# First norm of a two-layer diffusion backbone: token sums from the loaded x, root and reciprocal on 128x5, modulation by halves, first projection in parts

## The reference, cut to what matters

```
def adaln(cond, w, b):
    return jnp.split(jax.nn.silu(cond) @ w + b, 6, axis=-1)

def rms_norm(x, g):
    xf = x.astype(jnp.float32)
    xf = xf * lax.rsqrt(jnp.mean(xf * xf, axis=-1, keepdims=True) + EPS)
    return (xf * g.astype(jnp.float32)).astype(x.dtype)

def latent_layer(x, mod, cache, rows, cols, p):
    sh1, sc1, g1, sh2, sc2, g2 = mod
    h = rms_norm(x, p['norm1']) * (1 + sc1) + sh1
    ...
    x = x + g1 * (mixed @ p['w_out'])
    return channel_mlp(x, sh2, sc2, g2, p), (na_k, na_v, ckv, kpe, sk, sv)
```

## Time and profile before

| | us |
|---|---|
| median of 3 runs | 1737.93 |
| lowest, highest | 1737.55, 1741.01 |
| the profiled execution, its time | 1741.36 |
| its span in the trace | 1739.1 |
| mean granted TensorE clock, share of full speed | 0.966 |

### The profile page before, as it was taken

One profiled execution on the slowest core, in us unless ns is written; L12 is line 12 of the kernel. 1 busy time (PEld: TensorE's weight loads), 2 busy tenths in 40 slices (PEclk: granted clock), 3 DMA queues, 4 the chain that ended last, 5 costly groups with the idle time before them and its releaser, 6 DMA issues.

```text
span 1739.1 us, 28317 instructions
## 1 busy us (share of the span) xinstructions
PE 1610.1 (93%) x11686; PEld 1489.9 (86%) x11686; DVE 949.3 (55%) x1480; ACT 664.1 (38%) x1045; POOL 148.3 (9%) x107
## 2 busy tenths in 40 slices
PE   5878897899999999999988799978999999999998
PEld 3755895589999999999967569946999999999998
DVE  3653346856555545654584433497566456554553
ACT  4554533753422322232244454357433222332231
POOL 1002102520000000000010030064000000000000
PEclk9898998999999999999999899989999999999999
DMA  9440443311222222223534205341222222222211
GB/s 312 156 144 1 72 142 103 112 47 52 76 94 70 69 81 73 73 73 116 191 106 135 85 1 119 106 155 50 73 74 73 73 73 73 73 73 73 91 55 61
DMA packets 150856, 160.14 MB, mean 92 GB/s; under 512 B 16390, under 2 KB 132808, under 8 KB 150728
## 3 DMA queue, kind: packets, MB, share of 16 engines
q1 hardware_dynamic: 150024, 158.13, 29.7%
q10 hardware_dynamic: 576, 0.16, 0.0%
q0 software_dynamic: 128, 0.05, 0.0%
HBM read 153.41 MB, written 4.65 MB: 91 GB/s over the span
## 4 chain that ended last, share of the span: by engine, by line
PE 78%; DVE 11%; ACT 6%; issue 3%; DMA 1%; ACTq 0%; DVEq 0%; SPq 0%
PE ps L1552 33%; PE ps L1895 26%; PE ps L1645 10%; PE ps L1617 2%; PE ps L1669 2%; PE ps L1532 1%; DVE extrema L1306 1%; PE ps L1578 1%; ACT pt_c L788 1%; DVE extrema L1289 1%; PE ps L1722 1%; PE ps L1700 1%; DMA ada_own<-in_w_ada 1%; DVE mod L1147 1%; DVE w_lo L1134 1%
## 5 line engine op out<-in xcount | busy, mean ns | idle before, releaser
L788 ACT ACTIVATE w_hi<-w_raw 128x2048 fp32r<-128x2048 f32 (+1 forms) x90 | 169.9, 1887 | 333.8 <-PE ps L1552 324.3
L1348 DVE SCALAR_TENSOR_TENSOR xT<-ps,mod,xT 128x128 f32<-128x128 f32 (+2 forms) x432 | 190.0, 440 | 195.8 <-PE ps L1552 183.9
L1134 DVE TENSOR_TENSOR w_lo<-w_raw,w_hi 128x2048 fp32r<-128x2048 f32 (+1 forms) x90 | 203.1, 2257 | 140.4 <-ACT w_hi L788 138.9
L1895 PE MATMUL ps<-xa_hi,w_hi 128*128 128x320 f32 (+1 forms) x1024 | 236.1, 312 | 0.0
L1895 PE MATMUL ps<-xa_lo,w_hi 128*128 128x320 f32 (+1 forms) x1024 | 235.2, 311 | 0.0
L1895 PE MATMUL ps<-xa_hi,w_lo 128*128 128x320 f32 (+1 forms) x1024 | 235.1, 311 | 0.0
L1552 PE MATMUL ps<-z_hi,w_hi 128*128 128x320 f32 x1024 | 233.7, 310 | 0.9 <-DVE xT L1348 0.9
L1552 PE MATMUL ps<-z_lo,w_hi 128*128 128x320 f32 x1024 | 233.4, 309 | 0.0
L1552 PE MATMUL ps<-z_hi,w_lo 128*128 128x320 f32 x1024 | 233.3, 309 | 0.0
L1106 ACT ACTIVATE z_relu<-z_relu,sink_shift 128x128 f32<-128x128 f32 (+1 forms) x128 | 72.2, 564 | 307.0 <-DVE z_relu L1452 304.9
L1895 PEld LDWEIGHTS ps<-xa_hi,w_hi 128*128 128x128 f32 x1024 | 173.5, 189 | 0.3
(11 more groups left out here) (241 smaller groups left out, 2364.4 us busy)
## 6 DMA issues: line engine op xcount, KB each, us to landing
w_raw<-in_mlp_w SPq DMA_DIRECT2D x64, 1024.0 KB, 5.2
ada_own<-in_w_ada SPq DMA_DIRECT2D x54, 512.0 KB, 4.5
w_raw<-in_w_in SPq DMA_DIRECT2D x14, 1024.0 KB, 7.8
ada_mix<-in_w_ada SPq DMA_DIRECT2D x21, 512.0 KB, 7.8
ada_room<-in_w_ada SPq DMA_DIRECT2D x15, 512.0 KB, 8.9
w_raw<-in_w_out SPq DMA_DIRECT2D x8, 768.0 KB, 5.3
ada_first<-in_w_ada SPq DMA_DIRECT2D x6, 512.0 KB, 9.1
x_in<-in_x_sample SPq DMA_DIRECT2D x1, 2048.0 KB, 8.6
```

Source lines behind the costliest of these rows:

```text
L788: do(nc.scalar.activation(out, in_, ACT.Copy), sem)
L1134: do(V.tensor_tensor(w_lo[:, n % 2, 0:w], w_raw[:, n % 2, 0:w], f32(w_hi[:, n % 2, 0:w]), ALU.subtract), w_lo_ready)
L1348: do(V.scalar_tensor_tensor(dst, src, gate[:, m:m + 1], dst, ALU.mult, ALU.add), sem if last else None)
L1895: last = M.matmul(bank(b + a_, s1 - s0), w[r][:, k, c:c + P], x[:, k, s0:s1], start=k == 0 and q == 0, stop=k == KC - 1 and q == 2)
```

## The change

In layer 0 ACT squares each token tile of x as it was loaded (128 tokens by 1024 channels) with the sum along the row, so `tok_rstd` (128x5) holds each token's sum; no squares of `xT`, no additions and no matmul with ones are left there. In layer 1 the squares stay, but PE takes the partial sums as weights against one column of ones, 10 matmuls of 1 column. Mean, root and reciprocal then run on 128x5. PE spreads the result over the partitions (`spread_rstd`, 6 matmuls of a broadcast column against the identity), and ACT copies it out (`take_rstd`).

The 16 units are taken in the order scale 0 to 3, shift 0 to 3, scale 4 to 7, shift 4 to 7, with two PSUM banks for the sums in turn. h of chunks 0 to 3 waits for the first eight units alone; units 12 to 15 run between chunk 1 and chunk 2 of the projection, their turn between chunk 2 and chunk 3. The first weights are loaded before the ninth unit. The projection's banks are others, and the four units that followed it now stand behind the first tile of ckv. The diff, cut to its core:

```diff
-CQ_BANKS = (0, 1, 3, 7, 2)
+ADA_GROUPS = (2, 0, 3, 1)
+CQ_BANKS = (4, 5, 0, 6, 7)
...
+        FIRST_TICKS = [(None, ("unit", k)) for k in range(6)] + [(("turn", 0), ("unit", 6)), (None, ("unit", 7)), (("turn", 1), None)]
+        FIRST_TICKS += [(None, ("unit", k)) for k in range(8, 12)] + [(("turn", 2), None)]
+        FIRST_TICKS += [(None, ("unit", k)) for k in range(12, 16)] + [(("turn", 3), None)]
...
-            load_adas(0, range(AFTER_X))
-
-            sp.wait_ge(t_done, KC)
+            load_adas(0, range(8))
+            load_weights(0)
+            load_adas(0, range(8, AFTER_X))
+
+            sp.wait_ge(t_done, trans_ix.at[("x", KC - 1)] + 1)
+            sp.wait_ge(x_squared, NT)
             load_adas(0, range(AFTER_X, 16))
-            load_weights(0)
+            load_weights(1)
...
# ACT
+            def take_rstd(l):
+                i = acc_ix.at[(l, "rstd")]
+                act.wait_ge(m_done, i + 1)
+                do(nc.scalar.activation(rstds[0][:, :].rearrange("p (a n) -> p a n", a=2), acc_view(i), ACT.Copy), m_act)
+            def first_norm(l):
+                load_sqrt()
+                if l:
+                    for c in range(KC):
+                        act.wait_ge(y_read, (l * GROUPS - 1) * KC + c + 1)
+                        square_x(2 * l, c)
+                    ada_ticks(48 * l, range(8))
+                    root_x(2 * l)
+                else:
+                    ada_ticks(0, range(4))
+                    root_x(0)
+                take_rstd(l)
+                if l == 0:
+                    ada_ticks(0, range(4, 8))
+                    split_hi(0)
+                ada_ticks(48 * l, range(8, 13))
+                h_halves(2 * l, range(3))
+                ada_ticks(48 * l, range(13, 19))
+                h_halves(2 * l, range(3, KC))
...
-                act.wait_ge(acol_ready, nrm + 1)
                 for c in chunks:
+                    act.wait_ge(acol_ready, 3 * l + 1 + c // 4)
+                    act.wait_ge(mod_ready, 12 * l + 2 + 2 * (c // 4))
...
+            def square_tokens(t):
+                do(nc.scalar.activation(x_sq[:, :], x_in[:, t, :], ACT.Square, accum_out=tok_rstd[:, t:t + 1]), x_squared)
...
# DVE
             for l in range(DEPTH):
                 U = 45 * l
+                if l == 0:
+                    mean(0)
+                    invert(0)
+                ada_ticks(48 * l, range(7))
+                scales(2 * l, 0, 4)
                 if l:
                     mean(2 * l)
-                    ada_ticks(48 * l, range(6))
                     invert(2 * l)
-                    ada_ticks(48 * l, range(6, 18))
+                ada_ticks(48 * l, range(7, 9))
+                if l == 0:
+                    split_lo(0)
...
                 for c in range(KC):
+                    if c == 4:
+                        ada_ticks(48 * l, range(9, 14))
+                        scales(nrm, 4, 4)
+                    if c == 6:
+                        ada_ticks(48 * l, range(14, 19))
...
# POOL
-                pool.wait_ge(rstd_ready, nrm + 1)
+                pool.wait_ge(m_act, acc_ix.last_reader(acc_ix.at[(l, "rstd")])[1])
...
# PE
+            def first_norm(l):
+                if l:
+                    ada_ticks(48 * l, range(8))
+                    begin_acc((l, "sum1"))
+                    sums(l, "sum1")
+                    ada_ticks(48 * l, range(8, 11))
+                    pe.wait_ge(y_read, did["y"])
+                    spread_rstd(l)
+                    ada_ticks(48 * l, range(11, 14))
+                else:
+                    ada_ticks(0, range(6))
+                    spread_rstd(0)
+                    ada_ticks(0, range(6, 14))
+                project_cq(l, 45 * l, range(2))
+                ada_ticks(48 * l, range(14, 18))
+                project_cq(l, 45 * l, range(2, 3))
+                ada_ticks(48 * l, range(18, 19))
+                project_cq(l, 45 * l, range(3, KC))
...
-                project_cq(l, U)
+                first_norm(l)
+                project(l, U + 1, "ckv", range(1))
+                pe.wait_ge(p_read, proj_at[(l, "cq", NT - 1)] + 1)
+                pe.wait_ge(ada_reduced, 12 * l + 4)
                 ada_ticks(late, late_ticks(l, 1))
-                project(l, U + 1, "ckv")
+                project(l, U + 1, "ckv", range(1, NT))
```

More of the change, by code:

```diff
@@ L810, in ada_tick @@
                         act.wait_ge(ada_turned, u // 4)
-                    copy(ada_row[:, :], bank(ada_banks(first)[0]), ada_rows)
+                    copy(ada_row[:, :], bank(ada_acc_bank(first, unit[1])), ada_rows)
             def ada_ticks(first, ks):
@@ L1164, in mean @@
                 rstd = rstds[which]
-                i = acc_ix.at[(l, ("sum1", "sum2")[which])]
+                if which == 0:
+                    if l:
+                        i = acc_ix.at[(l, "sum1")]
+                        dve.wait_ge(m_done, i + 1)
+                        do(V.tensor_reduce(tok_rstd, bank(acc_banks(i), 2 * NT).rearrange("p (a t) -> p t a", a=2), AX_X, ALU.add),
+                           m_dve)
+                    else:
+                        dve.wait_ge(x_squared, NT)
+                    do(V.tensor_scalar(tok_rstd, tok_rstd, 1.0 / D, EPS, ALU.mult, ALU.add), mean_ready)
+                    return
+                i = acc_ix.at[(l, "sum2")]
                 dve.wait_ge(m_done, i + 1)
@@ L1591, in sums @@
                 rstd = rstds[nrm % 2]
+                if which == "sum1":
+                    out = bank(acc_banks(acc_ix.at[(l, which)]), 2 * NT)
+                    for a_, (x, ready, count) in enumerate(((rstd, sum_used, (KC - 2) * nrm), (sq[:, (KC - 1) % 2], sq_ready, KC * nrm))):
+                        pe.wait_ge(ready, count)
+                        for t in range(NT):
+                            at0 = NT * a_ + t
+                            last = M.matmul(out[:, at0:at0 + 1], x[:, P * t:P * t + P], ones[:, 0:1], start=True, stop=True,
+                                            skip_group_check=True)
+                    last.then_inc(m_done, 1)
+                    return
                 out = acc_view(acc_ix.at[(l, which)])
-                for x, ready, count in ((rstd[:, :], sum_used, (KC - 2) * (nrm + 1)),
-                                        (sq[:, (KC - 1) % 2, :], sq_ready, KC * (nrm + 1))):
+                for x, ready, count in ((rstd[:, :], sum_used, (KC - 2) * nrm),
+                                        (sq[:, (KC - 1) % 2, :], sq_ready, KC * nrm)):
                     pe.wait_ge(ready, count)
@@ L1599, in sums, with spread_rstd, project_cq @@
                 last.then_inc(m_done, 1)
-            def project_cq(l, n):
+            def spread_rstd(l):
+                begin_acc((l, "rstd"))
+                pe.wait_ge(tok_ready, l + 1)
+                b = acc_banks(acc_ix.at[(l, "rstd")])
+                for t in range(NT):
+                    for s, e in ((P * t, P * t + P),) if t != 2 else ((P * t, HALF), (HALF, P * t + P)):
+                        last = M.matmul(bank(b + s // HALF)[:, s % HALF:s % HALF + e - s],
+                                        tok_rstd[:, t:t + 1].broadcast_to([P, P]), ident[:, s - P * t:e - P * t],
+                                        start=True, stop=True, skip_group_check=True)
+                last.then_inc(m_done, 1)
+            def first_norm(l):
+                wait_read(trans_ix, did["t"] - 1, t_act, t_dve)
+                wait_read(trans_ix, did["t"] - 2, t_act, t_dve)
+                if l:
+                    ada_ticks(48 * l, range(8))
[5 more added lines that the diff above has]
+                    ada_ticks(48 * l, range(11, 14))
+                else:
+                    ada_ticks(0, range(6))
[6 more added lines that the diff above has]
+                project_cq(l, 45 * l, range(3, KC))
+            def project_cq(l, n, ks):
                 s = n % 2
```

146 lines of the change are left out of this document (62 added, 84 removed).

## The result

The changed kernel takes 1744.98 us (median of 19 runs, 1741.2 to 1750.06), the kernel before beside it 1737.93 (19 runs, 1734.55 to 1742.18). The ratio is 1.0035, 95% interval 1.0026 to 1.0044: about 6 us slower. The forecast was 1738.0 with a range of 1731.5 to 1743.5. The time lies outside the range, and the side it fell on had been given a chance of 0.30.

What follows compares the result with a forecast made beforehand. PE, busy for 93% of the span, was taken as the bound, so only its idle or half-clock stretches could pay. Layer 0 -3.7, layer 1 +2.9, ckv waits +0.9 gave +0.1 us: 1738.0, range 1731.5 to 1743.5.

Steps and rivals of the forecast that it cites:

- the lock: DVE instructions with two SBUF inputs and POOL's block each other on a shared port; a wait of 1.6 us per layer.
- Layer 0, start: Layer 0 up to the projection: without the 4.16 us reciprocal, PE starts at 41.6 instead of 51.16.
- Layer 0, chunks 0 and 1: First 30 projection matmuls of layer 0, some 20 at 0.213 us after idle PE: 5.4 us in all.
- Layer 0, tail: Layer 0 projection after the row copy, ACT setting the pace: 14.6 us, ending at 64.2, 3.7 us gained.
- Layer 1, start: Layer 1 up to the projection: PE starts at 897.6 instead of 900.90, 3.3 us earlier.
- Layer 1, projection: Layer 1, first to last projection matmul: 23.0 us instead of 16.9, ending at 920.6 instead of 917.8, 2.9 us lost.
- ckv: Behind the projection, ckv's first tile waits for the fourth copy of cq: 0.45 us lost in each layer.
- The sum: Both layers together: -3.7 + 2.9 + 0.9 = +0.1 us, predicting 1738.0.
- The gain stays: Rival: DVE and POOL hardly hinder each other, PE keeps full clock up to the projection; net -6.3, 1731.6 us; chance 0.26.
- The clock falls inside the projection: Rival: from chunk 3 on PE's waits drop the clock to half; net +5.8, 1743.7 us; chance 0.24.

Runs made afterwards that it cites:

- after_again: The changed kernel itself run once more with no edit; ratio to the kernel before 1.0031 (1.0019 to 1.0043).
- pool_late: The changed kernel with POOL's first two multiplications (chunks 2 and 3) held until the layer's first h_lo, both layers; ratio to the kernel before 1.0013.
- row3_late: The changed kernel with ACT's chunk 3 of h ahead of its copy of the fourth row, both layers; ratio to the kernel before 0.9980.
- units_ahead: The changed kernel with units 12 to 15 and ACT's copy of their row ahead of projection chunk 0, both layers; ratio to the kernel before 0.9966.
- both_ahead: units_ahead and sums_first combined, with ACT's copy of the fourth row behind the first two chunks of h; ratio to the kernel before 0.9950.
- all_three: both_ahead and pool_late combined; ratio to the kernel before 0.9966 (0.9950 to 0.9981).
- dve_all: both_ahead with POOL's multiplications of chunks 2, 3 and 5 given to DVE; ratio to the kernel before 0.9975.
- sums_first: The changed kernel with layer 1's sums of squares directly behind its sixth unit, root, mean and reciprocal moved forward too; ratio to the kernel before 1.0015.
- dve_all_ckv: dve_all with ckv's first tile not waiting for cq's fourth copy, its second only for the third copy; ratio to the kernel before 0.9967.

## Why the prediction was wrong, by its own steps

**The path and the lock were right. The sum failed because a wait in layer 0 and a half clock in layer 1 were missing from it, one of its figures does not add up, and the sizes that were off were nearly all off on the same side.**

- *Layer 0, start.* 42.4 instead of 41.6. The sum lets the first row copy follow the root's table at once. But PE began its first units only behind ACT's last copy, at 25.32, and at half clock (48 records in 5.21 us; in the kernel before 32 records took 1.93), so ACT waited for them, and the reciprocal came at 30.2 instead of 28.0:

```profile
29.08 0.60 ACT L804 ACTIVATE ada_row<-ps 128x512 f32<-128x512 f32 x1 [2.34 <-PE ps L1630]
```

  In after_again the first 32 records took as long (3.68 us) though the granted clock there was 1.00, so what slowed them stays open. The spreading, 1.53 instead of 2.3, and PE's turn and units, which ran beside ACT's copy, gave most of this back; the row copy ahead of `w_hi` ended 0.8 us late. The projection's start 8.7 us before the old one is real.
- *Layer 0, chunks 0 and 1.* 5.99 instead of 5.4: the first matmul took 0.35 us and the next 21 took 0.213 each, at half clock, where I took 20 of 30. In after_again it was 5.52.
- *Layer 0, tail.* The idle time of ACT (6.03, forecast 5.5), the addition beside POOL (1.50) and the row copy as pace setter were as forecast; from the copy's end 14.9 instead of 14.6. In all the projection gained 2.0 us and not 3.7.
- *Layer 1, start.* 1.4 us later than forecast in the first trace. Sums 2.32 (2.2), spreading 1.55 (1.3): 0.5 us together with hand-overs. Another 0.4 is a slip in adding up: from 892.0, two chunks of 2.33 and an `h_lo` of 1.16 make 897.8, and the prediction has 897.4. The rest, about 0.5, is how the lock fell. I took one piece blocked and one free in each chunk, 4.66 in all. But both pieces of chunk 0 were blocked, 3.73 us, and chunk 1's were free; all four took 4.92, and the first `h_lo` then waited 0.2 for chunk 0's `h_hi`. It ends at 898.83. pool_late shows that the lock is worth 2.6 us here, most of which the sum had.
- *Layer 1, clock.* This term was missing, and it is the largest single one: I had priced the clock for the projection only. In after_again, the same kernel, the two units and the spreading took 1.86 and 2.28 us instead of 1.00 and 1.55, and the start came at 16.6. These are the two rows, and behind them the spreading of row3_late, which also starts at 16.6:

```profile
885.81 1.86 PE ps L1630 x16
887.67 2.28 PE ps L1670 x12
```

```profile
883.47 2.64 PE ps L1670 x12
```

  Of the ten traces with the new start of layer 1, six have the spreading at half clock, 2.28 to 2.86 us (after_again, units_ahead, row3_late, both_ahead, all_three, dve_all), and four at full clock, 1.53 to 1.55 (changed, sums_first, pool_late, dve_all_ckv). It costs 1.6 us. The four traces with the old start all have 17.0. Against that, the three traces with the changed kernel's own start gain 2.0, 0.4 and 0.4 us, where 3.3 was forecast. Why the clock falls in one execution and not in another is not shown.
- *Layer 1, projection.* 23.6 and 23.8 us from first to last matmul instead of 23.0. Measured from the last square it ends 4.7 us later than before (38.6 against 33.9), in the second pair of profiles 7.2 (40.4 against 33.2), and not 2.9.
- *ckv.* The wait itself was 0.44, as forecast, but without it ckv's norm came 0.67 a layer earlier.
- *The sum.* At ckv's norms the two profiles give +4.2 and +5.3 us where I had +0.1; the runs gave +6.1 and +5.4. In the first pair layer 0 gives -1.4 at ckv's norm (forecast -3.7 and 0.45 for the wait) and layer 1 +5.4 (forecast 2.9 and 0.45): so the forecast missed by 1.8 us in layer 0 and by 2.0 in layer 1, in the second pair by 1.0 and 4.5, with the half clock ahead of layer 1's projection. The 0.1 to 1.9 us between the starts and the runs lie elsewhere.

**The rivals.** "The gain stays" fails on the lock, which pool_late takes away and then sees 2.6 us. "The clock falls inside the projection" gave nearly the right time (1743.7 against 1744.98) by the wrong mechanism, and being near is luck: half clock was paid ahead of the projection and in its first chunks, not in its tail. These windows of the changed kernel lie in the two tails; PE is busy for 2.79 and 2.02 of 5 us in the first of each pair, and the granted clock (third number from the end) stays 1.00:

```profile
55.00:60.00 5.00, 2.79 (x24) 2.59 (x23) 3.63 (x6) 3.83 (x7) 0.78 (x1) 1.00 0.64 214
60.00:65.00 5.00, 5.00 (x44) 5.00 (x43) 3.08 (x5) 4.18 (x7) 0.00 (x0) 1.00 0.00 0
...
910.00:915.00 5.00, 2.02 (x15) 1.84 (x15) 4.57 (x7) 2.28 (x4) 1.60 (x1) 1.00 0.81 272
915.00:920.00 5.00, 4.93 (x40) 4.93 (x41) 2.58 (x5) 4.77 (x8) 0.00 (x0) 1.00 0.00 1
```

The own range ended at +3 us. It had no room on that side for terms that can only add: a half clock ahead of the projection, and a wait for PE's first units.

**What stays open.** The starts explain 4.2 to 5.3 of about 6 us. For units_ahead and row3_late the median lies 2.8 and 3.8 us below what the starts say, beyond the interval. The granted clocks of their executions go with it: their means are 0.973 and 0.976, against 0.970 of the kernel before beside them (33 executions). Among those 33 the time falls by about 0.67 us per 0.001 of granted clock, which as an estimate makes 2.1 and 3.7 us, the size of both gaps. But sums_first, pool_late and dve_all, with means of 0.971 to 0.972, lie about 2 us above their starts. So it stays a correlation, and why these kernels should be granted more is open. both_ahead with ckv's wait taken out was not run.

## What to carry to other kernels

Work that is put into a product in parts costs what waits behind it on every engine, not its own length: four units of 1.9 us between chunks 1 and 2 cost 4 to 5 us, because a copy in ACT's order and a turn in front of PE's next chunk hung on them, while PE's idle 4 us just ahead of the product took them for nothing. When a chain in front is shortened, first look where the moved work finds PE idle, and in which order the other engines take its hand-overs. And add up the bounds of a sum with their signs: what can only be late must widen the range to one side.

## What the runs showed of the hardware

- DVE instructions with two SBUF inputs waited for POOL's multiplication whatever their own length: an addition of 128x8 took 1.50 instead of 0.17, pieces of 128 and 512 columns 1.75 and 1.98 instead of 0.36 and 0.76. The two pieces of one chunk each paid for one of two POOL instructions in a row; the chunk in one piece was not run.
- Holding POOL back paid where PE had slack at chunk 1 (2.6 us earlier start) and lost 2.3 and 1.6 us at the ckv norms where it had none.
- The same two units and spreading, 28 records on PE, took 2.55 us at a granted clock of 1.00 and about 4.1 where it fell to about 0.5 among them, in six of ten traces; one trace of a kernel can show either.
- The same instructions of one kernel took 794.1 or 795.4 us, and 796.4 or 800.7 us, in two executions, with other stretches at half clock. Its two spans differ by 6.1 us, so a difference of 2 us in a single pair of spans says nothing about a change.
